# Who casts the weight chunks: ScalarE in the mixer, VectorE in the feed-forward part, with three smaller moves beside it

## The chip, the cores and the metric

One Trainium2 chip, one of its cores. The metric is the device time of the whole program in microseconds (us), median over runs. Engines are named as in the profile: PE is TensorE, PEld its weight loads, DVE VectorE, ACT ScalarE, POOL GpSimd, SP SyncE, whose queue issues nearly all DMAs. The granted clock is the share of full speed at which TensorE was allowed to run.

## The reference

Two layers over 528 tokens (16 meta tokens and 512 inputs) of width 1024, in float32. Each layer is a mixer and a convolutional feed-forward part:

```python
for l in range(2):
    xn = rms_norm(h, norm1_g)                    # mixer
    proj = xn @ w_in                             # q, k, v, gates of three attentions
    out_a, out_b, out_c = fox(...), mla(...), sliding_window(...)   # 8 heads each
    y = einsum('blnc,ncd->blnd', stack(out_a, out_b, out_c), w_branch)
    h = h + sum(sigmoid(gates) * y, axis=2) @ w_o
    u = rms_norm(h, norm2_g) @ w_up              # feed-forward part, 1024 -> 5632
    c = conv_b + sum(conv_w[i] * shift(u, i))    # width 3, causal
    gate, val = split(c, 2)
    h = h + (silu(gate) * val) @ w_down          # 2816 -> 1024
return h[:, 16:]
```

## The kernel before

**Layout.** Activations stand transposed: 128 features on the partitions, the 528 tokens along the row (`T`), one such tile for each 128 features. Every product with weights is a chain of 128x128 weight blocks; there are 1080 blocks per layer, 2160 in all, and they lie in DRAM in the order in which TensorE uses them.

**Split products.** A float32 product is made of three: `gemm` multiplies the high part of the weights (cast to fp32r, `wh`) with the high and the low part of the activations (`xh`, `xl`), and the low part of the weights (`wl`) with the high part of the activations. The 528 columns are two halves of 264, in two banks of PSUM, so a block is 6 matmuls. In the last layer columns that nothing reads are left out (`two_before`, `real`): the last products (`dn`) have halves of 248 and 264.

**The weight stream.** Eight blocks are a chunk, 128x1024 float32, 512 KB; there are 270. SP loads a chunk into one of `RAW = 2` places of `raw`, VectorE casts it to `wh` (`high_part`), GpSimd subtracts in four pieces to get `wl` (`chunk_low`), and TensorE uses it (`weights`). There are `SPLIT = 3` places of `wh` and `wl`, and the cast of a chunk is issued `AHEAD = 2` chunks before its use: at block n, VectorE's `advance` casts chunk n/8 + 2, after waiting for its load and for TensorE to have started chunk n/8 (`s_start`).

**The order of the mixer.** `mixer_plan` writes out one list for each engine. The position in it is the number of the weight block (488 in a mixer, so 61 chunks), and the steps of attention, norms and gates are put at positions by hand (`ORDER`, `BEGIN`, `LAG`); at one position they go by rank, and the block comes last, with rank 9. Each engine executes its own list in order. After the list come `w_o` (64 blocks), `up` (352) and `dn` (176).

**Norms.** The sum of squares over features is a matmul with ones (`stat`), then ScalarE guesses the root and VectorE refines it (`newton`). The input of a layer is scaled by the norm's weights on VectorE (`scale_input`, into `tmp`), cast on ScalarE (`high_input`), and subtracted on VectorE (`low_input`). In the first layer TensorE adds up the squares itself: `first_stat(k)` ahead of each of the first eight blocks of tile `ff`, and ScalarE squares h tile k only when the statistic of tile k-2 is done. In the second layer VectorE adds the squares (`sum_square`), and one `stat` follows.

**Before w_o.** When the whole list is done, ScalarE casts the eight tiles of `merged` (`mh`) and VectorE subtracts all eight (`ml`); TensorE's first block of `w_o` waits for the first `ml`.

**The start.** SP issues the first two tiles of h, the first constants, chunk 0, the other h tiles, chunk 1, then the rest of the constants and chunks 2 and 3. VectorE ticks `ready_made` at the end of its preamble; ScalarE waits for it before its list.

## Time and profile before

| | |
|---|---|
| median of 3 runs | 2052.18 us (2051.9 to 2056.09) |
| time of the profiled execution | 2050.07 us |
| its span, first to last instruction | 2048.3 us |
| mean granted clock | 0.992 |
| TensorE busy | 1974.3 us, 96% |

The profiled execution's time is 1.8 us more than its span, and 2.1 us under the median. Busy TensorE is not TensorE at its peak, since the ends of matmuls are modelled; start-to-start distances in the timeline tell the rate. A group of instructions is a row with its count, its busy time and the mean of one, and then the idle time of its engine just before it with what ended it.

### The profile page before, as it was taken

The numbers are of one execution on the slowest core, as the hardware profiler recorded it, in microseconds if no ns is written. First come the engines' busy times: TensorE is split into PE (matmuls) and PEld (weight loads), VectorE is DVE, ScalarE is ACT, GpSimd is POOL, SyncE is SP. The second block draws the span as 40 slices with busy tenths as digits, with TensorE's granted clock in tenths as the row PEclk, the third lists the DMA queues.
The fourth block names the chain that finished last, engine by engine and source line by source line (L and its number), as shares of the span: only waits on it lengthen the run. The fifth ranks groups of instructions, "written<-read, shape, count | busy, mean of one in ns | idle before, by whom it ended". The sixth has DMA issues, their size and how long they took to land.

```text
span 2048.3 us, 37777 instructions
## 1 busy us (share of the span) xinstructions
PE 1974.3 (96%) x15080; PEld 1876.6 (92%) x15080; DVE 1154.7 (56%) x2137; ACT 766.3 (37%) x1483; POOL 1019.4 (50%) x1306
## 2 busy tenths in 40 slices
PE   7899999999999999999998999999999999999999
PEld 7888898888999999999997888988889999999999
DVE  5665466677455665652256654666774656656411
ACT  5455566555232222220034555665552232222100
POOL 5745544444444444455467555444443445444543
PEclk9999999999999999999999999999999999999999
DMA  4212111111233323323332121111112323232332
GB/s 154 56 50 63 52 44 61 45 50 52 63 105 93 93 83 94 93 83 104 93 115 63 43 63 53 52 52 52 52 42 73 115 83 102 85 100 87 103 94 93
DMA packets 44803, 156.35 MB, mean 76 GB/s; under 512 B 5010, under 2 KB 5266, under 8 KB 44628
## 3 DMA queue, kind: packets, MB, share of 16 engines
q1 hardware_dynamic: 44484, 153.71, 24.8%
q8 instruction: 120, 1.97, 0.4%
q14 instruction: 55, 0.45, 0.1%
q10 hardware_dynamic: 144, 0.22, 0.0%
HBM read 149.58 MB, written 4.26 MB: 75 GB/s over the span
## 4 chain that ended last, share of the span: by engine, by line
PE 80%; DVE 10%; ACT 4%; issue 3%; POOL 2%; DMA 0%; DVEq 0%; ACTq 0%; SPq 0%; POOLq 0%
PE ps L1294 22%; PE ps L1297 21%; PE ps L1299 21%; PE ps L1528 5%; PE ps L1304 3%; DVE osum L1906 2%; PE ps L1435 1%; PE ps L1474 1%; DVE rstd L1619 1%; DVE ps L1876 1%; POOL wl L789 1%; PE ps L1480 1%; PE ps L1500 1%; DVE square L1614 1%; ACT square L987 1%
## 5 line engine op out<-in xcount | busy, mean ns | idle before, releaser
L789 POOL TENSOR_TENSOR wl<-raw,wh 128x256 fp32r<-128x256 f32 x1080 | 797.8, 771 | 723.5 <-DVE wh L1598 714.0
L1294 PE MATMUL ps<-xh,wh 128*128 128x264 f32 (+1 forms) x2880 | 810.6, 303 | 4.9 <-POOL wl L789 2.7
L1297 PE MATMUL ps<-xl,wh 128*128 128x264 f32 (+1 forms) x2880 | 762.9, 285 | 0.0
L1299 PE MATMUL ps<-xh,wl 128*128 128x264 f32 (+1 forms) x2880 | 584.1, 284 | 0.0
L1294 PEld LDWEIGHTS ps<-xh,wh 128*128 128x128 f32 x2880 | 545.5, 189 | 29.0 <-issue 16.0
L1297 PEld LDWEIGHTS ps<-xl,wh 128*128 128x128 f32 x2880 | 545.8, 190 | 15.4 <-issue 6.7
L1299 PEld LDWEIGHTS ps<-xh,wl 128*128 128x128 f32 x2880 | 450.4, 190 | 0.0
L1598 DVE CAST wh<-raw 128x1024 fp32r<-128x1024 f32 x270 | 200.2, 742 | 180.7 <-PE ps L1294 166.2
L1297 PE MATMUL ps<-al,wh 128*128 128x264 f32 (+1 forms) x704 | 184.9, 283 | 0.0
L1294 PE MATMUL ps<-ah,wh 128*128 128x264 f32 (+1 forms) x704 | 183.6, 283 | 0.0
L1898 DVE TENSOR_TENSOR ps<-ps,cst 128x128 f32<-128x128 f32 (+6 forms) x240 | 70.9, 296 | 189.0 <-PE ps L1480 135.8
L1528 PE MATMUL ps<-pt,vx 128*128 128x256 f32 (+5 forms) x448 | 144.7, 403 | 0.8 <-ACT pt L1214 0.7
L1299 PE MATMUL ps<-ah,wl 128*128 128x264 f32 (+1 forms) x704 | 141.5, 282 | 0.0
L1294 PEld LDWEIGHTS ps<-ah,wh 128*128 128x128 f32 x704 | 132.4, 188 | 0.0
L1297 PEld LDWEIGHTS ps<-al,wh 128*128 128x128 f32 x704 | 132.4, 188 | 0.0
L1214 ACT ACTIVATE pt<-ps 128x256 f32<-128x256 f32 (+5 forms) x224 | 78.0, 362 | 113.5 <-DVE ps L1898 112.3
L1262 ACT ACTIVATE cv<-ps,prm 128x528 f32<-128x528 f32 (+1 forms) x44 | 34.6, 787 | 209.0 <-DVE ps L1955 209.0
L1294 PE MATMUL ps<-oth,wh 128*128 128x264 f32 (+1 forms) x384 | 108.9, 305 | 2.2 <-DVE ssum L1706 0.9
L1299 PEld LDWEIGHTS ps<-ah,wl 128*128 128x128 f32 x704 | 109.3, 188 | 0.0
L1955 DVE TENSOR_TENSOR ps<-ps,rstd 128x528 f32<-128x528 f32 (+1 forms) x88 | 62.0, 705 | 80.5 <-PE ps L1299 80.4
L1297 PE MATMUL ps<-otl,wh 128*128 128x264 f32 (+1 forms) x384 | 100.8, 283 | 0.0
L1435 PE MATMUL ps<-xk,xq 96*128 96x144 f32 (+9 forms) x272 | 75.4, 303 | 18.3 <-POOLq L886 7.7
(183 smaller groups left out, 3213.3 us busy)
## 6 DMA issues: line engine op xcount, KB each, us to landing
raw<-weights SPq DMA_DIRECT2D x270, 512.0 KB, 3.6
h<-tokens SPq DMA_DIRECT2D x4, 528.0 KB, 6.6
h<-tokens SPq DMA_DIRECT2D x8, 264.0 KB, 5.4
residual<-h SPq DMA_DIRECT2D x8, 264.0 KB, 4.7
h<-residual SPq DMA_DIRECT2D x8, 264.0 KB, 5.9
out<-h SPq DMA_DIRECT2D x8, 256.0 KB, 4.9
cst<-constants SPq DMA_DIRECT2D x1, 1008.0 KB
extra<-positions SPq DMA_DIRECT2D x17, 4.1 KB
```

The costliest lines, as they stand in the source:

```text
L789: ins = nc.gpsimd.tensor_tensor(wl[c % SPLIT][:, part], raw[:, c % RAW, part], wh[c % SPLIT][:, part].bitcast(F32), ALU.subtract)
L1214: ins = nc.scalar.activation(pt[0:nk, i, 0:nq], bank[0:nk, 0:nq], ACT.Exp)
L1294: a = nc.tensor.matmul(out, a_hi, x_hi[:, sl], start=first, stop=False)
L1297: nc.tensor.matmul(out, a_hi, x_lo[:, sl], start=False, stop=False)
L1299: ins = nc.tensor.matmul(out, a_lo, x_hi[:, sl], start=False, stop=last)
L1304: ins = nc.tensor.matmul(half(slot, j), lhs, rhs[:, j * TH:(j + 1) * TH], start=first, stop=last)
L1435: ins = nc.tensor.matmul(bank[:, col:col + nk], xq[rows, i, e, q], xk[rows, i, e, k0:k0 + nk], start=True, stop=True)
L1528: ins = nc.tensor.matmul(heads_out[:, c:c + nq], vals[0:nk, :], pt[0:nk, i, 0:nq], start=t == 0, stop=t == 4)
L1598: nc.vector.tensor_copy(wh[c % SPLIT][:, :], raw[:, c % RAW, :]).then_inc(s_hi, 1)
L1898: nc.vector.tensor_tensor(sc, sc, cst[0:nk, a:a + n], ALU.add).then_inc(scores_masked.sem, scores_masked.tick((l, j, e, t)))
L1906: nc.vector.reciprocal(osum[:, a:a + T // 4], osum[:, a:a + T // 4]).then_inc(dve_step.sem, dve_step.tick((l, "recip", j, q)))
L1955: nc.vector.tensor_tensor(src[:, skip:T], src[:, skip:T], rstd[:, skip:T], ALU.mult).then_inc(up_scaled.sem, up_scaled.tick((l, t)))
```

## The change

- In the mixer, ScalarE casts the chunks, at the block steps of its own list; in `w_o`, `up` and `dn` VectorE does, as before. The first chunk of each engine's turn waits for the other's last one. Chunks 0 and 1 are still cast by VectorE, and it also makes the low part of chunk 0.
- ScalarE scales and casts the norms' input in one activation straight from h, and VectorE makes the low part with one operation from h, the norm's weights and `xh`. `tmp` and its scaling on VectorE are gone, for norm 1 and norm 2.
- In the first layer ScalarE squares into `merged`, with no wait for TensorE; VectorE adds the squares, and one `stat` replaces the eight. The first constants are loaded after all of h and chunks 0 and 1.
- The casts of `merged` and their low parts go in between: tile d's at the step that ends the next product tile, and only the last after the list.
- In the last layer's `dn`, a block is three matmuls of 512 columns into one bank, where it was six of 248 and 264.

```diff
@@ SP
             for k in range(0, KD, 2):
                 sp.dma_start(h[:, k:k + 2, :], H[:, k:k + 2, :]).then_inc(s_hin[k // 2], 16)
-                if k == 0:
-                    sp.dma_start(cst[:, 0:CC_FIRST], CST[:, 0:CC_FIRST]).then_inc(s_first, 16)
-                    load(0)
-            load(1)
+
+                if k <= 2:
+                    load(k // 2)
+            sp.dma_start(cst[:, 0:CC_FIRST], CST[:, 0:CC_FIRST]).then_inc(s_first, 16)
@@ ScalarE
             def high_input(l, k):
-                act.wait_ge(scaled.sem, scaled.at(l, "n1", k))
-                copy(xh[:, k, :], tmp[:, k % 2, :]).then_inc(high_ready.sem, high_ready.tick((l, "n1", k)))
+                nc.scalar.activation(xh[:, k, :], h[:, k, :], ACT.Identity,
+                                     scale=prm[:, l, PC_N1 + k:PC_N1 + k + 1]).then_inc(
+                    high_ready.sem, high_ready.tick((l, "n1", k)))
+            def merged_cast(l, d):
+                act.wait_ge(gate_used.sem, gate_used.at(l, "sum", MLA, d))
+                copy(mh[:, d, :], merged[:, d, :]).then_inc(merged_high.sem, merged_high.tick((l, d)))
             for k in range(KD):
+                if k % 2 == 0:
+                    act.wait_ge(s_hin[k // 2], 16)
                 high_input(0, k)
-                if k >= 2:
-                    act.wait_ge(stat_ready.sem, stat_ready.at(0, "part", k - 2))
-                nc.scalar.activation(hsq[:, k % 2, :], h[:, k, :], ACT.Square).then_inc(
+                nc.scalar.activation(merged[:, k, :], h[:, k, :], ACT.Square).then_inc(
                     residual_squared.sem, residual_squared.tick((-1, "dn", k)))
                 for s in plan["act"]:
+                    if s[0] == "block":
+                        n = l * LB + n_blocks
+                        n_blocks += 1
+                        if n % BLK == 0:
+                            c = n // BLK + AHEAD
+                            if first:
+                                act.wait_ge(s_hi, c)
+                                first = False
+                            act.wait_ge(s_raw[c % RAW], 16 * (c // RAW + 1))
+                            if c >= SPLIT:
+                                act.wait_ge(s_start, c - SPLIT + 2)
+                            copy(wh[c % SPLIT][:, :], raw[:, c % RAW, :]).then_inc(s_hi, 1)
+                    elif s[0] == "done" and s[1].kind == "y":
+                        br, d = s[1].m
+                        if br == MLA and d != Y_LAST[0]:
+                            merged_cast(l, Y_LAST[Y_LAST.index(d) - 1])
@@ TensorE
+            def gemm_in_bank(n, out, x_hi, x_lo, first, last):
+                a_hi, a_lo = weights(n)
+                a = nc.tensor.matmul(out, a_hi, x_hi, start=first, stop=False)
+                if n % BLK == 0:
+                    a.then_inc(s_start, 1)
+                nc.tensor.matmul(out, a_hi, x_lo, start=False, stop=False)
+                return nc.tensor.matmul(out, a_lo, x_hi, start=False, stop=last)
                         if t.kind == "ff":
-                            if l == 0:
-                                first_stat(k)
                             pe.wait_ge(low_ready.sem, low_ready.at(l, "n1", k))
@@ VectorE
             def low_input(l, k):
                 dve.wait_ge(high_ready.sem, high_ready.at(l, "n1", k))
-                nc.vector.tensor_tensor(xl[:, k, :], tmp[:, k % 2, :], xh[:, k, :].bitcast(F32),
-                                        ALU.subtract).then_inc(low_ready.sem, low_ready.tick((l, "n1", k)))
+                nc.vector.scalar_tensor_tensor(out=xl[:, k, :], in0=h[:, k, :], scalar=prm[:, l, PC_N1 + k:PC_N1 + k + 1],
+                                               in1=xh[:, k, :].bitcast(F32), op0=ALU.mult, op1=ALU.subtract).then_inc(
+                    low_ready.sem, low_ready.tick((l, "n1", k)))
+            for k in range(KD):
+                low_input(0, k)
+                if k == 0:
+                    high_part(0)
+                    dve.wait_ge(s_hi, 1)
+                    nc.vector.tensor_tensor(wl[0][:, :], raw[:, 0, :], wh[0][:, :].bitcast(F32), ALU.subtract).then_inc(
+                        s_lo, 1)
+                elif k == 3:
                     high_part(1)
+                if k >= 4:
+                    sum_square(-1, "dn", k - 4)
+            for k in range(KD - 4, KD):
+                sum_square(-1, "dn", k)
                     if s[0] == "block":
-                        advance(l, n_blocks)
                         n_blocks += 1
```

## Rows read from the trace of the kernel before

**Rows 1.** The page: busy time of each engine, share of the span, instructions.
```profile
PE 1974.3 (96%) x15080; PEld 1876.6 (92%) x15080; DVE 1154.7 (56%) x2137; ACT 766.3 (37%) x1483; POOL 1019.4 (50%) x1306
```
**Rows 2.** Stretches, one in the first mixer, one in `up`: length, busy time by engine.
```profile
400.00:500.00 100.00, 94.77 (x668) 85.03 (x667) 74.93 (x156) 54.20 (x105) 46.12 (x52) 1.00 0.18 54
...
800.00:920.00 120.00, 120.00 (x984) 120.00 (x983) 71.25 (x102) 27.64 (x40) 58.73 (x83) 1.00 0.30 88
```
**Rows 3.** The chain of work that ended last, share of the span by engine.
```profile
PE 80%; DVE 10%; ACT 4%; issue 3%; POOL 2%; DMA 0%; DVEq 0%; ACTq 0%; SPq 0%; POOLq 0%
```
**Rows 4.** TensorE's waits: line, what it waited for, us in total, times, longest.
```profile
PE ps L1435 <- POOLq L886: 7.7, 3, 3.9
...
PE ps L1294 <- DVE ml L1916: 5.1, 2, 2.5
...
PE ps L1474 <- ACT ptm L1193: 4.7, 6, 1.0
```
**Rows 5.** Groups of instructions by line, shapes kept apart: busy us, mean ns.
```profile
L1598 DVE CAST wh<-raw 128x1024 fp32r<-128x1024 f32 x270 | 200.2, 742 | 180.7 <-PE ps L1294 166.2 <-DMA raw<-weights 13.3 <-DVE merged L1755 0.2
...
L1643 DVE TENSOR_TENSOR hsum<-hsum,sq 128x528 f32<-128x528 f32 x21 | 15.4, 735 | 2.1 <-ACT sq L1243 2.0
...
L970 ACT ACTIVATE xh<-rawt 128x528 fp32r<-128x528 f32 x32 | 20.4, 636 | 123.0 <-DVE rawt L1628 122.5 <-DVE rawt L1936 0.6
...
L1262 ACT ACTIVATE cg<-ps,prm 128x528 f32<-128x528 f32 x22 | 17.4, 793 | 45.8 <-DVE ps L1955 45.8
...
L977 ACT ACT_TABLE_LOAD x12 | 15.4, 1283 | 0.2
...
L1075 ACT ACTIVATE gsb<-gsb 128x1056 f32<-128x1056 f32 x12 | 12.8, 1081 | 8.9 <-DVE gsb L1739 8.9
...
L789 POOL TENSOR_TENSOR wl<-raw,wh 128x256 fp32r<-128x256 f32 x1080 | 797.8, 771 | 723.5 <-DVE wh L1598 714.0 <-POOL xq L802 2.5 <-POOL xk L877 1.0
```
**Rows 6.** Timeline of the start: start us, length us, idle time before in brackets.
```profile
5.32 1.27 DVE L1628 TENSOR_SCALAR rawt<-h,prm 128x528 f32<-128x528 f32 x2 [4.02 <-DMA h<-tokens]
...
7.08 0.69 DVE L1598 CAST wh<-raw 128x1024 fp32r<-128x1024 f32 x1 [0.48 <-DMA raw<-weights]
...
12.02 0.56 PE L1294 MATMUL ps<-xh,wh 128*128 128x264 f32 x1 [2.75 <-POOL wl L789]
...
14.79 1.96 PE L1304 MATMUL ps<-sq,cst 128*128 128x264 f32 x4
...
26.17 1.30 DVE L1598 CAST wh<-raw 128x1024 fp32r<-128x1024 f32 x2
...
33.14 0.39 PE L1294 MATMUL ps<-xh,wh 128*128 128x264 f32 x1 [0.80 <-DVE krt L1718]
...
34.70 1.16 PE L1304 MATMUL ps<-sq,cst 128*128 128x264 f32 x4
```
**Rows 7.** Timeline of TensorE: blocks of the last `dn`, then a 512-column product.
```profile
1990.14 0.28 PE L1294 MATMUL ps<-ah,wh 128*128 128x248 f32 x1
...
1992.99 0.28 PE L1294 MATMUL ps<-ah,wh 128*128 128x248 f32 x1
...
424.47 0.39 PE L1474 MATMUL ps<-xq,xk 97*128 97x512 f32 x1
...
425.17 0.29 PE L1294 MATMUL ps<-xh,wh 128*128 128x264 f32 x1
```
**Rows 8.** Second layer's `w_o`: its first matmul, and the stretch just after.
```profile
1620.05 0.35 PE L1294 MATMUL ps<-mh,wh 128*128 128x250 f32 x1 [2.53 <-DVE ml L1916]
...
1621.00:1624.40 3.40, 3.40 (x18) 3.40 (x17) 3.40 (x7) 0.00 (x0) 0.00 (x0) 0.51 0.99 317
```
**Rows 9.** Timeline around two of the mixer's stalls of TensorE.
```profile
319.95 0.39 PE L1474 MATMUL ps<-xq,xk 97*128 97x256 f32 x1 [0.83 <-ACT ptm L1193]
...
432.04 1.36 DVE L1598 CAST wh<-raw 128x1024 fp32r<-128x1024 f32 x1
...
434.16 0.18 PE L1474 MATMUL ps<-xq,xk 97*16 97x16 f32 x1 [0.75 <-ACT pt L1214]
```

More of the change, by code:

```diff
@@ L446, in build @@
     lrstd = hsum
-    tmp, hsq = rawt, sq
+    hsq = sq
     vt = sb("vt", [P, TK])
@@ L822, in _ @@
             pool.sem_inc(zeroed.sem, zeroed.tick((0, 0)))
-            for c in range(AHEAD):
+            for c in range(1, AHEAD):
                 chunk_low(c)
@@ L1233, in _ @@
                             heads_copied.sem, heads_copied.tick((l, j, e)))
-                for d in Y_LAST:
-                    act.wait_ge(gate_used.sem, gate_used.at(l, "sum", MLA, d))
-                    copy(mh[:, d, :], merged[:, d, :]).then_inc(merged_high.sem, merged_high.tick((l, d)))
+                merged_cast(l, Y_LAST[-1])
                 def square_residual(which, k):
@@ L1246, in _ @@
                 for k in range(KD):
+                    act.wait_ge(residual_updated.sem, residual_updated.at(l, "wo", k))
+                    nc.scalar.activation(xh[:, k, :], h[:, k, :], ACT.Identity,
+                                         scale=gain[:, l, PC_N2 + k:PC_N2 + k + 1]).then_inc(
+                        high_ready.sem, high_ready.tick((l, "n2", k)))
                     square_residual("wo", k)
-                    act.wait_ge(scaled.sem, scaled.at(l, "n2", k))
-                    copy(xh[:, k, :], tmp[:, k % 2, :]).then_inc(high_ready.sem, high_ready.tick((l, "n2", k)))
                 logarithms()
@@ L1575, in _ @@
                     slot = DN_SLOTS[m]
+                    if real:
+                        if m % 2 == 0:
+                            pe.wait_ge(up_freed.sem, up_freed.at(l, 2 * FT - 4 + m // 2))
+                        out = last_bank(m)
+                        for k in range(FT):
+                            if m == 0:
+                                pe.wait_ge(act_low.sem, act_low.at(l, k))
+                            ins = gemm_in_bank(l * LB + n_blocks, out, ah[:, k, real:T], al[:, k, real:T], k == 0,
+                                               k == FT - 1)
+                            n_blocks += 1
+                        ins.then_inc(tile_ready.sem, tile_ready.tick((l, "dn", m)))
+                        continue
                     if m < 4:
@@ L1598, in high_part @@
                 nc.vector.tensor_copy(wh[c % SPLIT][:, :], raw[:, c % RAW, :]).then_inc(s_hi, 1)
+            turns = {"mixer": True}
             def advance(l, i):
@@ L1602, in advance @@
                 if n % BLK == 0:
+                    if turns["mixer"]:
+                        dve.wait_ge(s_hi, n // BLK + AHEAD)
+                        turns["mixer"] = False
                     high_part(n // BLK + AHEAD)
```

74 lines of the change are left out of this document (33 added, 41 removed).

## The prediction

> **What bounds the kernel now.** I read the page first: TensorE is busy 1974.3 us of a span of 2048.3 [rows 1], so all its idle time together is 74.0 us, and nothing that the change does to another engine can give more than that unless it shortens TensorE's own work. The stretches come next [rows 2]: in `up` TensorE is busy 120.00 of 120.00 us, with VectorE at 59%; in the mixer it is busy 94.77 of 100, with VectorE at 75% and ScalarE at 54%. So the feed-forward part is bound by TensorE's instructions alone, and the engines that feed TensorE matter only in the two mixers and at the start. The chain that ended last says the same: 80% TensorE, 10% VectorE, 4% ScalarE, 2% GpSimd [rows 3]. The waits of TensorE [rows 4] name no single cause: the reader should see many stalls of about 1 us, behind VectorE, ScalarE and GpSimd alike, and one that the change addresses by name, 5.1 us in two stalls behind `ml`. The timeline is then read at the start, at `w_o` and in the last `dn`.
>
> **The start.** Before, h is there at 5.32 and chunk 0 at 7.08; GpSimd makes chunk 0's low part, and TensorE's first block begins at 12.02 [rows 6]. After, ScalarE makes `xh` 0 straight from h (0.64 as a plain cast, 0.79 as the activation with a scale per partition [rows 5]; I take 0.7), VectorE subtracts (0.74) at about 6.8, casts chunk 0 (0.74), and makes its low part: twice the columns of a 0.735 us operation, less its fixed part, 1.3 us. That ends at 8.8: 3.2 us earlier. The next condition is block 16, which needs chunk 2. Its cast waits for `ready_made`, behind VectorE's whole preamble. Counted from 8.8: seven low parts, eight additions and the cast of chunk 1 at 0.74 are 11.8 us, then 0.5 for the gains: 21.1. Overlap of neighbours takes some off, GpSimd working on chunk 1 beside it puts some on; I take 21.2. ScalarE casts chunk 2 (1.05, priced below) and GpSimd makes it low in 4 x 0.771 = 3.1 us [rows 5]: TensorE can start block 16 at about 25.4. TensorE itself is ready earlier: from 8.8, 16 blocks at 0.72 us and one statistic of about 1.0 are 12.5, and the first blocks run at half speed, as before, where the first two took 14.79 - 12.02 = 2.77 us [rows 6], 1.3 more than two at 0.72. Twice that, 2.6, gives 23.9. Before, chunks 2 and 3 were cast at 26.17, and block 16 began at 33.14, for eight statistics stood in the way [rows 6]. That is 7.7 us earlier.
>
> What is late next is the root of norm 1. ScalarE reaches it after the casts of chunks 2 and 3, at 23.5; a table load of 1.28 and six operations of 0.64 (copy, logarithm, exponential, square, then copy and square of the first tile) are 5.1 us [rows 5] and end at 28.7, where TensorE does that tile's statistic. Before, that statistic began at 34.70 [rows 6]. So from here the whole schedule runs 6.0 us earlier, and TensorE waits there some 2 us that it did not wait before. The stall behind GpSimd (L886, two of nearly 4 us, one in each layer [rows 4]) stays: its chain moves with the statistic. I take 6.0 for the start. The lower bound is 3.2, the first block's gain alone; the upper 8.
>
> **w_o.** Each layer's first block of `w_o` waits 2.5 us for `ml`, since VectorE begins the eight subtractions only when its list is done. After, the first seven are done in between, and only the last is behind the list; TensorE needs that one 14 blocks, 10 us, later. The added work per product tile of 4 blocks (2.9 us) on VectorE is one subtraction of 0.7, beside two operations of 0.7, so it does not pace. Gain 5.1 us [rows 4]. In the second layer the stall is followed by 3.4 us at a granted clock of 0.51 [rows 8], which is half speed, 1.7 us of work lost. Without the stall I take 1.3 of it back. Together 6.4; bounds 5.1 and 6.8.
>
> **The last dn.** Four blocks take 1992.99 - 1990.14 = 2.85 us, 0.7125 a block, six matmuls [rows 7]. Three matmuls of 512 columns in a row are in the trace too: from 424.47 to the next instruction of another kind at 425.17, 0.70 us. The columns are the same, 1536, so only what each matmul costs beside its columns is saved: 0.0125 us by this row. Resolution is 0.01 at both ends, and the three there are of other products. 176 blocks x 0.0125 = 2.2 us. Nothing is the lower bound. From above: 248 and 264 columns at 2.4 GHz are 0.640 us for the block, so 0.0725 stands beside the columns; halving it gives 0.036, or 6.4 us. I take 2.8, near the row. The Trainium skill (TensorE: Matmul & The Clock Gate, on the 56 ns gap) puts that cost at about 2.5 ns for a matmul; by it the sum would be 176 x 3 x 0.0025 = 1.3 us, an estimate. The trace has more beside the columns than that, so the two disagree.
>
> **The casts.** VectorE loses 122 casts, two mixers of 61, at 0.742 us: 90 us of work [rows 5]. ScalarE gains them. The nearest row is an activation without a scale per partition over 1056 columns, 1.081 us; for 1024 I take 1.05, so 128 us. The stretch of 100 us in [rows 2] holds some ten of them: ScalarE goes from 54% to about 65%, VectorE from 75% to 67%; neither becomes the bound by its sum. What counts is who stands in line behind a cast. ScalarE's cast at block n waits for TensorE to start block n, as VectorE's did, and then exponentials, key copies and root guesses wait up to 1.05 us; on VectorE, masks, maxima and refinements stop waiting 0.74 us, or 1.36 as in [rows 9]. For a gain: the cast of 1.36 us at 432.04 is followed by the stall of 0.75 at 434.16 [rows 9]; I count seven like it in both layers, about 5 us. For a loss: the stalls behind `ptm` (4.7 us in six) have ScalarE as the late engine already, busy with the copies of the next job; the one at 319.95 [rows 9] is the start of the job at block 250, two blocks behind the chunk boundary 248, so its 0.83 becomes up to 1.9. Some five places per layer are like that. A stall also brings half clock with it in places, as in [rows 8]. I take 2 us slower for both mixers, between 6 faster (all seven, and a clock drop) and 12 slower (1.05 us exposed at ten of the 122 casts, and one clock drop).
>
> **Norm weights inside the cast.** Norm 2 and the second layer's norm 1 lose 24 scalings on VectorE, and ScalarE's casts get 0.1 longer. TensorE has no stall there, in either place; one block of cover, 0.7 us, is more than what any link changes. Nothing. Had that cover gone, the low part would come at most 0.2 us later per tile.
>
> **The sum.** -6.0 - 6.4 - 2.8 + 2.0 = -13.2 us. Against the profiled execution's 2050.07 that is 2036.9. Its time was 2.1 us under the median of 2052.18, and a median of the changed kernel may lie above its profile too, so I take half of that on top: 2038.
>
> **Rivals.**
> - *The start gives little.* If the preamble on VectorE is stretched by GpSimd or by late DMAs (the first constants now come after 3.4 MB), `ready_made` slips, with it chunk 2, and only the first block's 3.2 us are kept, or less. 2040 to 2043. For it: 16 operations in a row on one engine. Against: chunk 0 was there 1.8 us after h [rows 6]; at that pace the five pieces of half a megabyte ahead of the constants are there by 15, before they are wanted.
> - *The casts on ScalarE help.* If removing VectorE's casts mends the seven stalls and ScalarE has room, the mixers give 6 us: 2029. For it: the same cast takes 0.69 us at 7.08 and 1.36 at 432.04 [rows 6, 9], and what it waits for there, GpSimd may wait for elsewhere. Against: GpSimd is on 2% of the chain [rows 3]. The Trainium skill (SBUF — State Buffer, on the engine ports) says that GpSimd and a VectorE copy in its two-port mode lock each other out, and that ScalarE's ports are its own; by it the move frees both engines, and it speaks for this rival. That the cast's length varies agrees with it.
> - *ScalarE becomes the late engine of the attention.* Three banks rotate among scores and maxima, so a score tile that ScalarE frees 1.05 us late holds up the third one behind it. The other parts give 15.2 us; it decides against the change once the mixers lose more than that and 4 us, 0.16 us for each of the 122 casts. At 0.2 they lose 24: 2050.07 - 15.2 + 24 = 2059. For it: stalls behind ScalarE exist already [rows 4]. Against: ScalarE would still idle a third of the mixer [rows 2].
> - *The wide matmuls give nothing*, at the same rate per column: 2040.
>
> **How the numbers follow.** The forecast, 2032 to 2043 with its own bounds, has 0.55 (the first and fourth rivals' milder forms lie in it). The helping casts: 0.2, 2024 to 2032. A weak start and exposed casts together in part: 0.12, 2043 to 2048. ScalarE late: 0.13, 2048 and up, more than half of it beyond 2052+4. The range 2024 to 2049 leaves 0.06 below and about 0.12 above. Within 0.2% is 2048.1 to 2056.3, about what a measurement of this kernel can tell from no change: 0.07. Faster: 0.86. Slower: 0.07.
>
> **What would show it.** First block of TensorE near 8.8, and the first tile's statistic near 28.7. No idle time before `w_o`'s first matmul, and no half clock behind it in the second layer. Start-to-start of a block in the last `dn` between 0.68 and 0.71. ScalarE's casts near 1.05 us; TensorE's idle time between 70 us and the end of each mixer within 2 us of before. If the waits of TensorE behind `pt`, `ptm` and `sq` grow by more than 15 us together, the prediction is wrong in its sign.

## The result, and the profile after

The changed kernel takes 2068.23 us (median of 5 runs, 2067.23 to 2072.54); the kernel before, run beside it, 2051.9 us. The ratio is 1.0083, with a 95% interval from 1.0066 to 1.0099: 16 us slower, where the prediction had 14 us faster. It is wrong in its sign, and 19 us beyond its range.

The profiled execution took 2067.81 us, with a span of 2066.0, against 2048.3 before. Its page, busy time by engine, answers to [rows 1]; under it the stretches of [rows 2]:

```profile
PE 1976.0 (96%) x14524; PEld 1854.0 (90%) x14524; DVE 1067.4 (52%) x1992; ACT 885.3 (43%) x1605; POOL 1012.2 (49%) x1302
```
```profile
400.00:500.00 100.00, 93.37 (x651) 83.99 (x650) 64.55 (x137) 61.64 (x112) 43.88 (x48) 0.98 0.15 45
800.00:920.00 120.00, 120.00 (x983) 120.00 (x983) 70.70 (x101) 27.62 (x40) 58.89 (x84) 1.00 0.31 93
```

VectorE did lose 87 us and ScalarE did gain 119. In the mixer ScalarE is busy 62% and VectorE 65%, nearly as forecast, and neither is full. `up` is as it was. What differs is TensorE in the mixer: 93.37 us instead of 94.77, at a granted clock of 0.98 instead of 1.00. Here are its waits (line, what it waited for, us in total, times, longest), to set against [rows 4]:

```profile
PE ps L1343 <- DVE rawt L1801: 13.2, 10, 2.5
...
PE ps L1464 <- POOLq L889: 7.4, 2, 3.8
PE ps L1503 <- ACT ptm L1222: 6.9, 6, 1.7
...
PE ps L1464 <- ACT xk L973: 6.7, 2, 3.4
...
PE ps L1503 <- ACT ptm L1225: 4.5, 6, 1.1
```

The 5.1 us behind `ml` are gone. `ptm` has 11.4 us instead of 5.6, `xk` 6.7 instead of 3.0, `rawt` 13.2 instead of 9.0: many small growths, behind ScalarE and behind VectorE.

**Where the time went.** I set matching instructions of TensorE against each other, above all the statistics (line 1304 before, 1343 after) and the first matmul of each chunk. After minus before: -4.1 us at the first tile's statistic (30.60 against 34.70), +10.5 at the end of the first mixer, +7.8 behind its `w_o`, +7.8 up to the end of the first `dn`, +11.3 at block 24 of the second layer, +24.3 at the end of the second mixer, +20.1 behind its `w_o`, +17.7 at the end of the span. So the start gave 4.1, the two `w_o` 6.9 and the last `dn` 2.4, 13.4 us together, where 15.2 were forecast. The two mixers took 31, where 2 were forecast.

**The start.** The timeline answers to [rows 6] (start us, length us, idle time before in brackets):

```profile
5.49 1.28 ACT L1004 ACT_TABLE_LOAD   x1 [5.49 <-DMA h<-tokens]
6.78 0.73 ACT L1004 ACTIVATE xh<-h,prm 128x528 fp32r<-128x528 f32 x1
...
9.04 1.22 DVE L1725 TENSOR_TENSOR wl<-raw,wh 128x1024 fp32r<-128x1024 f32 x1
...
10.41 0.56 PE L1324 MATMUL ps<-xh,wh 128*128 128x264 f32 x1 [10.41 <-DVE wl L1725]
...
12.98 5.02 POOL L792 TENSOR_TENSOR wl<-raw,wh 128x256 fp32r<-128x256 f32 x4 [6.15 <-DVE wh L1640]
...
13.84 1.24 DVE L1675 SCALAR_TENSOR_TENSOR xl<-h,prm,xh 128x528 fp32r<-128x528 f32 x1
...
23.50 2.00 ACT L973 ACTIVATE wh<-raw 128x1024 fp32r<-128x1024 f32 x2 [7.33 <-DVE nsink L1736]
...
25.52 1.28 ACT L980 ACT_TABLE_LOAD   x1
...
27.56 0.36 PE L1324 MATMUL ps<-xh,wh 128*128 128x264 f32 x1 [2.43 <-POOL wl L792]
...
30.60 1.16 PE L1343 MATMUL ps<-sq,cst 128*128 128x264 f32 x4 [1.34 <-ACT sq L1058]
```

There is a table load that the forecast did not have. It stands in front of ScalarE's first activation, and so behind the wait for h; it ends at 6.78. The first block begins at 10.41 instead of 8.8. While GpSimd makes the low part of chunk 1 (5.02 us instead of 3.1), VectorE's operations with two inputs take 1.24 us instead of 0.76, so the small tiles are ready at 23.5 instead of 21.2, and the rest of the chain moves with them.

**w_o and the last dn.** The first matmul of the second layer's `w_o` has no idle time before it, and where [rows 8] had a clock of 0.51 the clock is 1.00:

```profile
1641.81 0.28 PE L1324 MATMUL ps<-mh,wh 128*128 128x250 f32 x1
```
```profile
1642.00:1646.00 4.00, 4.00 (x36) 4.00 (x35) 3.40 (x5) 0.65 (x1) 0.44 (x1) 1.00 0.85 276
```

In the last `dn` six blocks of three matmuls go from 1995.00 to 1999.19, 0.698 us a block, where [rows 7] had 0.7125:

```profile
1995.00 0.39 PE L1335 MATMUL ps<-ah,wh 128*128 128x512 f32 x1
...
1999.19 0.39 PE L1335 MATMUL ps<-ah,wh 128*128 128x512 f32 x1
```

**The casts.** By groups, ScalarE's cast has the forecast length, the casts left to VectorE are shorter than in [rows 5], and GpSimd's low parts are as long as before (774 ns, 771 before):

```profile
L792 POOL TENSOR_TENSOR wl<-raw,wh 128x256 fp32r<-128x256 f32 x1076 | 799.4, 774 | 774.7 <-DVE wh L1640 434.0 <-ACT wh L973 333.3 <-POOL xq L805 1.9
...
L973 ACT ACTIVATE wh<-raw 128x1024 fp32r<-128x1024 f32 x122 | 128.5, 1054 | 59.0 <-PE ps L1324 50.4 <-DVE nsink L1736 7.3 <-DMA raw<-weights 0.4
...
L1640 DVE CAST wh<-raw 128x1024 fp32r<-128x1024 f32 x148 | 102.6, 693 | 140.4 <-PE ps L1335 64.1 <-PE ps L1324 64.0 <-DMA raw<-weights 12.2
```

So the length of one cast was forecast rightly. The mixers' loss must come from where the casts stand.

### The profile page after: what moved, and what is told of

It reads as the page before. It is cut to its first block and busy times, and to the rows that moved or that the text cites. A ratio compares the mean times of both kernels' runs of the same rounds, so it can differ in the third digit from the quotient of the medians.

```text
span 2066.0 us, 36684 instructions
## 1 busy us (share of the span) xinstructions
PE 1976.0 (96%) x14524; PEld 1854.0 (90%) x14524; DVE 1067.4 (52%) x1992; ACT 885.3 (43%) x1605; POOL 1012.2 (49%) x1302
## 5 line engine op out<-in xcount | busy, mean ns | idle before, releaser
L1640 DVE CAST wh<-raw 128x1024 fp32r<-128x1024 f32 x148 | 102.6, 693 | 140.4 <-PE ps L1335 64.1
L973 ACT ACTIVATE wh<-raw 128x1024 fp32r<-128x1024 f32 x122 | 128.5, 1054 | 59.0 <-PE ps L1324 50.4
L1503 PE MATMUL ps<-xq,xk 97*16 97x16 f32 (+17 forms) x288 | 79.6, 294 | 16.5 <-ACT ptm L1222 6.9
L1327 PE MATMUL ps<-al,wh 128*128 128x264 f32 x352 | 93.0, 285 | 0.0
L1324 PE MATMUL ps<-ah,wh 128*128 128x264 f32 x352 | 92.9, 284 | 0.0
L1961 DVE RECIPROCAL osum<-osum 128x132 f32<-128x132 f32 x96 | 88.5, 953 | 8.1 <-ACT oraw L973 7.8
L1343 PE MATMUL ps<-sq,cst 128*128 128x264 f32 (+1 forms) x224 | 63.8, 411 | 17.8 <-DVE rawt L1801 13.2
```

The source lines that it names most:

```text
L973: return nc.scalar.activation(out, in_, ACT.Copy)
L1324: a = nc.tensor.matmul(out, a_hi, x_hi[:, sl], start=first, stop=False)
L1327: nc.tensor.matmul(out, a_hi, x_lo[:, sl], start=False, stop=False)
L1343: ins = nc.tensor.matmul(half(slot, j), lhs, rhs[:, j * TH:(j + 1) * TH], start=first, stop=last)
L1503: nc.tensor.matmul(out, xk[rows, i, e, keys], xq[rows, i, e, q], start=True, stop=False)
L1640: nc.vector.tensor_copy(wh[c % SPLIT][:, :], raw[:, c % RAW, :]).then_inc(s_hi, 1)
```

## The experiments

The theories at first: A, ScalarE's 1.05 us per cast makes it the late engine. B, several parts lose together. C, the cast's wait for TensorE, standing in ScalarE's list, holds back what is behind it. Below, "boundary" is TensorE's first matmul on a new chunk, every eight blocks, and a "stretch" is the time from one boundary to the next, named by its first block.

**1. Casts back on VectorE** (`e1_dve_casts`: the changed kernel without this one part).
```diff
-  ScalarE, in the mixer: copy(wh[c % SPLIT], raw[c % RAW]) at each boundary
+  VectorE: advance(l, n_blocks) at each "block" of its list, as before the change
```


> The changed kernel with the mixer's chunks cast by VectorE again, at VectorE's own block steps; all else as in the change. Theory A (ScalarE is the late engine of the attention, and the 122 casts on it are the whole loss): the mixers return to what they took before, so 27 us come back, 2041 us, and TensorE's idle time in each mixer falls by about 8 us. Theory B (the loss is of several parts: squares and norms on ScalarE at the start, interleaved casts of merged too): less than 15 us come back, 2053 us or more.

Measured 2040.02 us, ratio to the kernel before 0.9938 (0.9915 to 0.9961). The parts that were left gain 11 us, and both mixers are within 3 us of before, as theory A had it. The other parts do not hurt: B falls.

**2. Casts alone** (`e2_act_casts_only`: the kernel before with this one part).
```diff
+  ScalarE, in the mixer: the cast at each boundary
-  VectorE: advance(l, n_blocks) in the mixer
```


> The kernel before with one part of the change: the mixer's chunks cast by ScalarE. Theory A: all the loss is here, without the gains: 27 us slower than before, 2078 us. Theory B: no more than 12 us slower, 2063 us.

2083.24 us, ratio 1.0157 (1.0126 to 1.0188), 32 us slower where A had 27. Both ways round the casts cost 28 to 32 us, 0.23 to 0.26 us for each of the 122.

**3. The wait alone** (`e5_wait_only`: as 1, and ScalarE waits at each boundary for TensorE's start, but casts nothing).
```diff
+  if n % BLK == 0 and c >= SPLIT:
+      act.wait_ge(s_start, c - SPLIT + 2)
```


> As the run with the casts back on VectorE, but ScalarE keeps its wait for TensorE's start of the chunk at each boundary, and does nothing there. Theory C (the wait is the harm): 10 us or more slower than the run without the wait. Theory A: within 3 us of it.

2043.65 us, 3.6 us more than 1: just beyond A's 3 us and far from C's 10. The wait by itself is an eighth of the loss.

**4. The cast two and four blocks later** (`e3_late`, `e8_late4`: the changed kernel with `n % BLK == 2`, `== 4`).
```diff
-  if n % BLK == 0:
+  if n % BLK == 2:        # e8_late4: == 4
```


> The changed kernel, ScalarE's cast of a chunk put two blocks later in its list (at n % 8 = 2), so that TensorE has started the chunk that the cast waits for before ScalarE comes to it. Theory C (the harm is the wait in ScalarE's queue: 50 us of ScalarE's idle time end with TensorE starting a block, and what stands behind waits too): half or more of the loss goes, 2055 us or less. Theory A (the harm is the 1.05 us of work itself, wherever it stands): within 5 us of the changed kernel, 2063 to 2073.

> The changed kernel with ScalarE's casts four blocks behind the boundary. ScalarE has the same 128.5 us of casts, but no wait for TensorE in its queue, and GpSimd's low part is 2.9 us later. The cast two blocks behind gave 2058.8. If the wait and what stands next to the boundary is what costs, 2048 to 2060; if ScalarE's time costs wherever it stands, 2060 to 2070; if the casts come too late for the next chunk (1.1 of 5.8 us of cover are left for cast and low part, 4.2 us, before the boundary), TensorE waits behind wl and it is above 2070.

2058.79 us and 2078.88 us. The first lies between the forecasts of A and C and settles nothing by itself: three of its ten runs took about 2052 us and the other seven 2057.7 to 2060.5, and the profiled one, 2052.06, is of the three. ScalarE has the same work in both. Here are the mixers' stalls of TensorE by releaser, both layers, each from its block 24 on, summed from the timeline:

```
us of idle TensorE      ScalarE  VectorE  GpSimd's queue   all
before                   17.9     26.8        7.7          52.5
after                    32.0     28.2        7.4          67.7
1: casts on VectorE      19.0     26.5        7.7          53.2
4: two blocks later      21.8     25.2       11.7          59.6
4: four blocks later     14.9     22.3       37.1          75.5
5: busy, no cast         23.1     27.9        7.2          58.2
6: VectorE, 1 later      18.8     29.6       11.0          59.4
```

("all" has 0.8 and 1.2 us behind GpSimd's own operations too, in the two kernels of run 4.)

With the cast four blocks late the stalls behind ScalarE are even fewer than before, so theory A as it stood loses ground: 128 us of work more on ScalarE cost nothing behind ScalarE where they stand in another place. It is not settled by this, since TensorE waits so long for others here that ScalarE may catch up meanwhile; `e11_spared` settles it (run 8). The time is above 2070, as the third forecast had it, but not for its reason: TensorE hardly waits behind `wl`. Instead GpSimd's list, which waits for each cast, is late with what stands behind the low part:

```profile
PE ps L1464 <- POOLq L889: 37.0, 9, 6.8
```

**5. ScalarE busy, no cast moved** (`e6_busy`: as 3, and then five copies of 128x3 into a scratch tile that nobody reads).
```diff
+  act.wait_ge(s_start, c - SPLIT + 2)
+  for i in range(5):
+      copy(waste[:, 3 * i:3 * i + 3], prm[:, 0, 0:3]).then_inc(s_waste, 1)
```


> Left as in the version with all casts on VectorE (2040.0 us), but at each block boundary of the mixer ScalarE waits for TensorE's start, as for a cast, and then does five copies of 128x3 (by its small operations about 0.2 us each, 1.0 us together), which nobody waits for. VectorE casts and GpSimd's low part stay where they were. If what costs is ScalarE's time alone (the copies, exponentials and root guesses behind it come 1 us later), this gives most of the loss: 2060 to 2068. If it is the later cast that pushes GpSimd's low part onto VectorE's work, or the tables and masks that VectorE now reaches earlier, this stays near the kernel with the wait alone, 2043.7: 2042 to 2050.

2049.67 us: 9.6 more than 1, at the upper edge of the second forecast and far below the first. The wait and ScalarE's time at the boundary are a third of the loss, and 3.6 of the 9.6 are the wait's, by run 3. But the substitute is weaker than it was meant to be. Each copy lasts 0.19 us, and they overlap: all 610 keep ScalarE busy for 70.3 us, 0.58 at each of the 122 boundaries, where a cast takes 1.05.

```profile
L975 ACT ACTIVATE waste<-prm 128x3 f32<-128x3 f32 x610 | 70.3, 192 | 59.0 <-PE ps L1326 50.7 <-DVE nsink L1734 7.3
```

**6. VectorE casts one block later** (`e7_vector_late1`).
```diff
-  advance(l, n_blocks)                      # casts at n % BLK == 0
+  if n % BLK == 1:
+      high_part(n // BLK + AHEAD)
```


> All casts on VectorE, but in the mixers one block (0.72 us) later than the boundary, so that GpSimd's low part begins some 0.7 us later than with the casts at the boundary, and ScalarE has none of it. If the later low part collides with VectorE's work at bad places, the mixers lose 5 us or more: 2045 to 2055. If ScalarE's time is all of it, no change beyond 3 us from 2040.0: 2037 to 2043.

2050.24 us: 10.2 more than 1, with nothing on ScalarE. In the mean over the 122 boundaries the cast ends 2.42 us behind the boundary in 1, 2.92 in the changed kernel, 3.06 here. A later cast costs by itself. It does not cost at the same places, though: 4.4 us of the loss stand in the stretch from block 40, both layers together, where TensorE waits longer for GpSimd's queue, and there the changed kernel loses nothing.

**7. Both together** (`e13_busy_late`: 5 and 6 in one kernel).

> Both substitutes together: ScalarE waits at the boundary and does 0.96 us of copies that nobody waits for (alone 9.6 us slower than 2040.0), and VectorE casts one block late (alone 10.2 us slower), so that the cast ends 3.1 us behind the boundary, as in the changed kernel. If ScalarE's hold and the later low part are the two halves of the loss and add up, 2059 to 2064; if they act in the same places and strengthen each other, up to 2070; if one hides the other, 2050.

2061.23 us, 21 more than 1: the two add up (9.6 + 10.2). The sum is three quarters of the loss with no cast on ScalarE, but it is not three quarters rebuilt: 4.5 us of it are again at block 40. What the substitutes do at the places where the changed kernel loses is in run 8.

**8. Where the loss is made.** I cut the traces at the boundaries. Of 61 stretches a layer most are the same to 0.05 us in the changed kernel and in 1; these are the five with the largest differences in both layers (us over 1, first and second layer):

```
stretch of block     120          288          312          328          352          all 122
after            0.93  2.54   2.31  2.24   3.49  3.43   0.94  0.91   0.87  0.92       28.3
e10_five         1.09  1.12   2.31  3.30   1.96  3.41   0.95  0.92   0.87  0.93       16.4
e11_spared      -0.16 -0.15  -1.03  1.46   0.02  0.01   0.01 -0.01   0.01  0.00       -1.9
```

and in six stretches (blocks 32, 56, 144, 240, 336, 376) the changed kernel is faster, by up to 0.7 us each. Some stretches differ as much in one layer alone: 3.5 us at block 248 of the first and 2.9 at block 192 of the second, of which 0.7 and 1.0 are idle time and the rest a granted clock of 0.79 and 0.90 instead of 1.00, and 1.9 and 1.6 at blocks 8 and 16 of the second, which come below. Of the 28.3 us, 18.3 are idle time of TensorE, and 10.0 the same work at a lower clock. So the next two kernels divide the casts by place. `e10_five`: ScalarE casts at these five places only, ten of the 270 casts. `e11_spared`: VectorE keeps 18 casts of each mixer, ScalarE takes 43.
```diff
+  BY_SCALAR = {15, 36, 39, 41, 44}          # e11_spared: set(range(61)) less 18 places
+  ScalarE: at a boundary k in BY_SCALAR, wait for the cast before it if that was VectorE's, and cast
+  VectorE: the same for all others
```


> From the version with all casts on VectorE (2040.0 us), ScalarE takes only five of the 61 casts of each mixer: those begun at blocks 120, 288, 312, 328 and 352. Cut at the chunk boundaries, the trace of the changed kernel is longer than that version's in these stretches by 0.9, 2.3, 3.5, 0.9 and 0.9 us in the first layer and 2.6, 2.2, 3.4, 0.9 and 0.9 in the second, 18.5 us together. If each loss is made where its cast stands, these ten casts alone give it: 2056 to 2061. If the loss comes from ScalarE's total load, ten of 122 casts give a twelfth of 28 us, 2.3: 2040 to 2044.

> The complement, with more spared: VectorE keeps the 18 casts of each mixer whose stretch was longer by some 0.2 us or more in either layer, ScalarE takes the other 43, 86 in all. If the losses are local, what is left are the gains, in the stretches of blocks 32, 56, 144, 240, 336 and 376 (0.4, 0.5, 0.7, 0.7, 0.3, 0.6 us a layer) and two waits more at each change of hands: 2033 to 2040. If ScalarE's load as such costs, 86 of 122 casts give 70% of 28 us: 2060.

2059.65 us and 2034.34 us, ratios 1.0040 (1.0025 to 1.0055) and 0.9920 (0.9905 to 0.9935), both as forecast for a local loss. Ten casts cost 19.6 us in the medians (16.4 in the trace, which is of the shortest run); 86 casts at other places cost nothing, and that kernel has the lowest median measured here. The other 26 casts stayed with VectorE in both kernels. The loss is local. It is not a matter of load; by groups, `e11_spared`:

```profile
L974 ACT ACTIVATE wh<-raw 128x1024 fp32r<-128x1024 f32 x86 | 90.7, 1055 | 35.3 <-PE ps L1324 34.6
```

TensorE's idle time in a stretch tells more than its length, since the clock is not in it. Where nothing was changed it repeats to about 0.02 us between kernels (us, first and second layer, worked out from the timeline):

```
stretch of block       120         288         312         328         352      8, second
1                  0.15 0.26   1.42 1.53   0.45 0.65   0.75 0.80   0.00 0.00     1.16
3: wait            0.20 0.33   1.42 1.52   1.29 1.35   0.75 0.80   0.00 0.00     1.17
5: wait, copies    0.77 0.94   1.42 1.52   1.85 1.92   1.17 1.20   0.13 0.17     1.87
6: VectorE later   0.46 0.57   1.70 1.80   0.39 0.45   0.74 0.79   0.00 0.00     1.16
7: both            1.05 1.19   1.71 1.81   1.85 1.92   1.15 1.20   0.12 0.17     1.87
after              1.08 1.18   3.33 3.38   2.39 2.45   1.64 1.67   0.60 0.64     3.05
```

At blocks 328 and 352 only ScalarE's time acts: the wait and the later cast do nothing, copies of 0.58 us give up to half of what the cast gives, and TensorE waits for `pt` and for `vx`, which stand behind it. At block 120, where it waits for `ptm`, the copies give more than half and the later cast the rest. At block 288 ScalarE's time does nothing and the later cast a little. At block 312 and at block 8 the cast gives more than its length.

**9. What acts at block 288.** In the kernel of 1, VectorE casts 0.54 us behind the boundary, and of VectorE's chain of six operations for the next tile, a refinement of two steps and four products, only the first meets GpSimd's low part:

```profile
374.32 2.80 POOL L792 TENSOR_TENSOR wl<-raw,wh 128x256 fp32r<-128x256 f32 x4 [9.25 <-DVE wh L1630]
...
376.58 1.10 DVE L1650 SCALAR_TENSOR_TENSOR square<-ssum,square 128x528 f32<-128x528 f32 x1
...
377.72 0.71 DVE L1653 SCALAR_TENSOR_TENSOR rstd<-square,rstd 128x528 f32<-128x528 f32 x1
...
378.56 0.75 DVE L1862 SCALAR_TENSOR_TENSOR q<-rawt,gain,rstd 64x528 f32<-64x528 f32 x1
...
379.32 0.70 DVE L1865 TENSOR_TENSOR q<-krr,rstd 32x528 f32<-32x528 f32 x1
380.05 0.77 DVE L1862 SCALAR_TENSOR_TENSOR q<-rawt,gain,rstd 64x528 f32<-64x528 f32 x1
...
380.83 0.70 DVE L1865 TENSOR_TENSOR q<-krr,rstd 32x528 f32<-32x528 f32 x1
```

In the changed kernel ScalarE is at its root guess when the boundary comes, and casts 2.73 us behind it. The low part then lies on that chain:

```profile
381.32 1.05 ACT L973 ACTIVATE wh<-raw 128x1024 fp32r<-128x1024 f32 x1
...
382.16 0.70 DVE L1664 SCALAR_TENSOR_TENSOR square<-ssum,square 128x528 f32<-128x528 f32 x1
...
382.45 4.45 POOL L792 TENSOR_TENSOR wl<-raw,wh 128x256 fp32r<-128x256 f32 x4 [11.85 <-ACT wh L973]
382.89 1.12 DVE L1667 SCALAR_TENSOR_TENSOR rstd<-square,rstd 128x528 f32<-128x528 f32 x1
...
384.13 1.03 DVE L1875 SCALAR_TENSOR_TENSOR q<-rawt,gain,rstd 64x528 f32<-64x528 f32 x1
...
385.17 1.14 DVE L1878 TENSOR_TENSOR q<-krr,rstd 32x528 f32<-32x528 f32 x1
386.34 1.13 DVE L1875 SCALAR_TENSOR_TENSOR q<-rawt,gain,rstd 64x528 f32<-64x528 f32 x1
...
387.48 1.53 DVE L1878 TENSOR_TENSOR q<-krr,rstd 32x528 f32<-32x528 f32 x1
...
389.95 0.56 PE L1464 MATMUL ps<-xk,xq 96*128 96x264 f32 x1 [3.33 <-ACT xk L973]
```

The chain begins 3.56 us behind the boundary in both kernels. Its six operations take 6.65 us instead of 4.73 and it ends 1.9 us later, which is all that TensorE's idle time grew by; the rest of the stretch's 2.31 is the clock. GpSimd's four take 4.45 instead of 2.80. Both sides slow each other; ScalarE's `xk`, which TensorE is said to wait for, is only the last link. The Trainium skill (SBUF — State Buffer, on the two separate sides) says that a VectorE operation with two inputs in SBUF and a GpSimd operation that reads SBUF lock each other out for a whole instruction; these rows agree, with 0.70 become 1.12 where a GpSimd piece of 0.7 us is in the way.

The kernel of run 6 has no cast on ScalarE, and its low part begins 2.28 us behind this boundary, between 1.31 in 1 and 3.85 in the changed kernel. It meets two operations of the chain:

```profile
376.24 3.74 POOL L792 TENSOR_TENSOR wl<-raw,wh 128x256 fp32r<-128x256 f32 x4 [8.41 <-DVE wh L1630]
...
378.26 1.12 DVE L1653 SCALAR_TENSOR_TENSOR rstd<-square,rstd 128x528 f32<-128x528 f32 x1
...
379.50 1.03 DVE L1864 SCALAR_TENSOR_TENSOR q<-rawt,gain,rstd 64x528 f32<-64x528 f32 x1
```

The chain ends 0.29 us later than in 1, and TensorE's idle time is 0.28 us longer. So the collision without ScalarE lengthens this stall; how much it gives at 3.85 us behind the boundary is read from the rows of the changed kernel only.

`e14_one_late3` has all casts on VectorE, but this one three blocks later:
```diff
+  if n_blocks // BLK == 36:
+      if n % BLK == 3: high_part(n // BLK + AHEAD)
+  else:
       advance(l, n_blocks)
```


> All casts on VectorE (2040.0 us), but the one of block 288 in each layer three blocks later, so that GpSimd's low part begins some 3.5 us behind the boundary, as with the cast on ScalarE (3.97), and not 1.42. If the later low part is the cause at that place, the stretch from block 288 to 296 gets 1 to 2.3 us longer in each layer, VectorE's two refinements and four products there take 1.0 to 1.5 us instead of 0.7, and the whole is 2042 to 2045. If ScalarE's own time is the cause there, no change: 2039 to 2041, apart from one cast of 0.7 us in VectorE's chain.

2041.27 us (2039.91 to 2043.77), the stretch 1.15 and 0.71 us longer, its idle time 0.75 and 0.70. The cast came later than meant, 6.6 us behind the boundary and inside the chain, so the first operation missed the low part and the last one met it:

```profile
378.07 0.70 DVE L1650 SCALAR_TENSOR_TENSOR square<-ssum,square 128x528 f32<-128x528 f32 x1
...
381.13 0.69 DVE L1630 CAST wh<-raw 128x1024 fp32r<-128x1024 f32 x1
...
381.85 0.77 DVE L1867 SCALAR_TENSOR_TENSOR q<-rawt,gain,rstd 64x528 f32<-64x528 f32 x1
381.90 3.82 POOL L792 TENSOR_TENSOR wl<-raw,wh 128x256 fp32r<-128x256 f32 x4 [15.33 <-DVE wh L1630]
382.63 1.13 DVE L1870 TENSOR_TENSOR q<-krr,rstd 32x528 f32<-32x528 f32 x1
```

The last operation is 0.43 longer than in 1, the first 0.40 shorter, and the cast itself takes 0.72: 0.75 together, the growth of the idle time. The one collision took the place of the other. So this run shows that a cast inside the chain costs its length; it does not test the later low part, and the 1.9 us were not rebuilt in this way.

**10. What acts at block 312.** With all casts on VectorE, ScalarE has loaded the tanh table and done the first tanh before the boundary. In the changed kernel the cast stands ahead of them in its list and waits there:

```profile
409.63 1.06 ACT L973 ACTIVATE wh<-raw 128x1024 fp32r<-128x1024 f32 x1 [3.27 <-PE ps L1324]
...
410.71 1.28 ACT L1104 ACT_TABLE_LOAD   x1
...
412.00 2.06 ACT L1104 ACTIVATE gsb<-gsb 128x1056 f32<-128x1056 f32 x2
...
416.16 2.10 PE L1343 MATMUL ps<-sq,cst 96*128 96x264 f32 x4 [2.39 <-DVE rawt L1801]
```

3.27 us of waiting, in which a load and a tanh would have fitted, and then all of it on the path to `rawt`. The table of run 8 divides it: over 1, the wait alone gives 0.84 us of idle time in the first layer and 0.70 in the second, with copies of 0.58 us behind it 1.40 and 1.27, with the cast 1.94 and 1.80. The same pair stands at block 8 of the second layer, ahead of the root of its first norm, where in 1 the load was done before the boundary:

```profile
1054.17 1.06 ACT L973 ACTIVATE wh<-raw 128x1024 fp32r<-128x1024 f32 x1 [3.05 <-PE ps L1324]
1055.25 1.28 ACT L980 ACT_TABLE_LOAD   x1
```

TensorE's idle time there is 3.05 us instead of 1.16 (1.17 with the wait alone, 1.87 with the copies), and the next eight blocks run at a clock of 0.80 instead of 1.00, 1.6 us more. `e16_tanh_first` is `e10_five` with this one cast moved behind the next tanh:
```diff
+  k == 39: keep the cast for later
   nc.scalar.activation(gates, gates, ACT.Tanh, scale=0.5)
+  cast it here
```


> The version with ScalarE's five casts per mixer (2059.7 us), but its cast of block 312 stands behind the next tanh instead of ahead of it. The tanh's gate is there before TensorE reaches block 312, so the table load (1.28) and tanh (1.08) go into ScalarE's wait. If the wait in the list is the cause at that place, the stretch from block 312 to 320 loses what it had gained (2.0 and 3.4 us): 2053 to 2056. If the cast's 1.05 us as such is the cause, at most 0.5 us a layer: 2058.5 to 2060.

2050.80 us (2047.06 to 2056.24), 8.9 less than `e10_five` (2055.84 to 2061.24) and more than was forecast. The stretch lost all it had gained (1.96 to -0.06, 3.41 to -0.19), 5.6 us in both layers, and the cast itself is still ScalarE's. The profiled executions don't show the medians' difference: that of `e10_five` was its shortest run, this one the longest of its own, and in it the stretches of blocks 88, 120 and 248, where nothing was changed, are up to 2.9 us longer. So the stretch is the evidence here; the median is more than it gives.

**11. The start, and a best version.** `e9_table_first` is 1 with the table of logarithms loaded at the head of ScalarE's list; `e12_six_table` gives ScalarE in addition the six casts where the changed kernel was faster; `e15_spared_table` is `e11_spared` with the table first.
```diff
   act.dma_start(prm[:, :, :], PRM[:, :, :]).then_inc(s_prm, 16)
+  logarithms()
```


> All casts on VectorE, and ScalarE loads the table of logarithms at the head of its list, before it waits for h. The load of 1.28 us at 5.49 goes into the shadow of h's transfer and the second load, before the root of norm 1, is gone. If both lie on the path: first block of TensorE 1.3 us earlier and the first tile's statistic 1.3 to 2.5 earlier, 2037.5 to 2039. If the path there is VectorE's and GpSimd's (chunk 1 and 2), only 0 to 1.3 us: 2038.7 to 2040.

> The version with the table loaded first (2036.6 us), and ScalarE takes only the six casts of each mixer in whose stretch the changed kernel was faster. If those gains are local too, 2 x 3.2 us less: 2030.2, range 2028 to 2034. If they came from a cast elsewhere, or each change of hands costs as much as it gives, 2035 to 2041.

> ScalarE takes 43 of the 61 casts of each mixer (2034.3 us with them), and its first table load stands at the head of its list (3.4 us less in the version where VectorE casts all). If start and mixers are independent: 2031, range 2029 to 2033. If the preamble's shift changes what meets in the mixers: 2033 to 2037.

2036.63, 2034.78 and 2036.01 us. The table first gives 3.4 us in the medians, but less than that is its own: in the trace TensorE's first block begins at 9.41 and its block 16 at 26.58, both 0.8 us earlier than in 1, where 1.3 were forecast, and the first tile's statistic at 28.53, 1.2 earlier. The rest of the traces' difference is 3.1 us at blocks 88 and 192 of the first layer, with the same idle time and a higher clock. The other two were expected at 2030 and 2031 if the gains added up. They did not; `e15_spared_table` lies in its second forecast. The six local gains are there in `e12_six_table` (up to 0.6 us each), but they are given back elsewhere. Windows over the same eight blocks (248 to 256 of the first layer), first in `e9_table_first`, then in `e12_six_table`:

```profile
308.95:322.07 13.12, 12.00 (x86) 10.34 (x84) 5.27 (x12) 9.57 (x25) 7.99 (x10) 1.00 0.26 82
```
```profile
310.24:326.49 16.25, 14.86 (x85) 12.56 (x84) 5.46 (x12) 9.80 (x25) 9.01 (x11) 0.79 0.22 67
```

Idle time is 1.1 and 1.4 us; the work went from 12.00 to 14.86 us, with the granted clock at 0.79 instead of 1.00. Four versions stand between 2034 and 2037 us, and their ranges overlap; `e11_spared` has the lowest median, 2034.34, 17 us under the kernel before, and no run tells the four apart.

## Why the prediction was wrong

**The step that failed** is the price of the casts for both mixers, 2 us, and its bound "between 6 faster ... and 12 slower (1.05 us exposed at ten of the 122 casts, and one clock drop)". The two mixers lost 31 us, 28 of them by the casts (run 1). The bound takes the cast's own length as the most that a place can lose. That holds at blocks 120, 328 and 352, where TensorE's idle time grew by 0.6 to 0.9 us, and at block 248, the place that the prediction names, where its 0.83 became 1.53. It fails elsewhere, since three things go with the cast that I had priced at nothing or nearly so:
- *The wait moves too.* I wrote that ScalarE's cast waits for TensorE as VectorE's did, and named what is behind it, but took the cast's length as the delay. At block 312 it waited 3.27 us, and a table load of 1.28 and a tanh of 1.09 came behind it: 1.9 us of idle time in each layer, shown by moving the one cast (run 10). At block 8 of the second layer it was 1.9 us again.
- *The cast comes when ScalarE comes to it.* At block 288 it starts 2.2 us later than VectorE's. GpSimd's low part follows it and meets VectorE's chain: 1.9 us of idle time in each layer. That the one cast does it is shown by `e10_five`, where it is as large; that it is the collision is read from the rows of run 9, and run 6 shows the collision without ScalarE at 0.3 us. The prediction said nothing of GpSimd's new hours.
- *Clock.* The mean granted clock fell from 0.992 to 0.986, 12.6 of the 28 us over the version with VectorE's casts (0.014 of a span of 2066.0 is 28.9 us, 0.008 of 2037.5 is 16.3); by stretches it is 10.0, and the other 18.3 are idle time. I had one drop, under 2 us.

That the bound counts ten places, and that ten casts made 19.6 of the 28 us, is luck: the ten were taken from stalls behind `ptm`, and only block 120 of the five is one of those.

**The rivals.** "ScalarE becomes the late engine of the attention" had the sign, the place and nearly the time (2059), with 0.13, and its price of 0.2 us per cast was measured at 0.23. As a matter of steady load it is refuted: 86 casts cost nothing. In places it is there: TensorE's waits behind `ptm` and `pt` went from 10.3 to 18.5 us in the mixers, and ScalarE's time alone gives part of that (run 5). "The casts on ScalarE help" is right at six places a layer, which give 0.2 to 0.7 us each. The rule that spoke for it, that the move frees VectorE and GpSimd from each other (the Trainium skill, SBUF — State Buffer, on the two separate sides), changed nothing in the mean: GpSimd's pieces took 774 ns, 771 before.

**The sign I would have read.** I had said that waits behind `pt`, `ptm` and `sq` growing by over 15 us would show it. They grew by 8 in the mixers (13.4 to 21.8), and the sign turned all the same: `rawt`, `xk` and `vx` took 10 more, and the clock the rest.

**The start** was forecast at -6.0 and measured at -4.1, in its bounds. Its first block came 1.6 us earlier, not 3.2. Two terms were missing: the table load behind the wait for h (1.28, of which run 11 gives back 0.8), and the stretch of VectorE's operations to 1.24 beside GpSimd's 5.02 us, which the rival of a weak start had in words. Block 16 began at 27.56 instead of 25.4, the statistic at 30.60 instead of 28.7.

**w_o** gave 2.7 and 4.2, 6.9 together, against 6.4: a tenth above its upper bound, but right in both its pieces, the stall and the clock behind it. **The last dn** gave 2.4 against 2.8; 0.698 us a block is just under the 0.70 of the row, and 176 x 0.0145 is 2.6. **Norm weights inside the cast** cost nothing in the feed-forward part, as said. In the second layer's first stretches 3.5 us went, which the prediction put at nothing. They belong to the casts, since ScalarE's casts of blocks 0 and 8 now stand ahead of the layer's root: in `e10_five` and `e11_spared`, where VectorE makes these, they are not there.

**The chances** add up to 1.00 without the 0.06 that the prediction gives to a time below 2024.

**What stays open.** At block 288 no run made the low part as late as the changed kernel has it without ScalarE's cast, so 1.6 of the 1.9 us of idle time rest on the rows alone. At blocks 120, 328 and 352 the cause is read from the substitutes, at about half the length of a cast; there, too, no single cast was moved. What made the granted clock fall in one kernel and not in another is not known: the stalls do not tell it, since it also changed between kernels with the same idle time.

## What to carry to other kernels

An instruction that is moved to another engine takes its waits along, and in a list that runs in order a wait costs what stands behind it. So price a move place by place: when does the new engine reach it, what is behind it, and who starts when it ends. A load that fits on average can cost 1% at ten places, and the cut at fixed work (chunk boundaries) finds these places in two traces, if idle time and clock are told apart in each piece. Moving the casts only where they are harmless gave the lowest median here. And a substitute that shall take an engine's time has to be measured itself: five copies of 0.19 us kept ScalarE for 0.58, not 0.96.

## What the runs showed of the hardware

The same eight blocks with the same idle time, 1.2 us, took 11.85 us of work at a granted clock of 1.00 in `e10_five` and 14.79 at 0.79 in `e16_tanh_first` (blocks 248 to 256 of the second layer, whose casts VectorE makes in both); stretches of blocks 88, 192, 248 and 280 move by 1.5 to 3 us between kernels in this way. Gains of half a microsecond at a stall are below that, and should be looked for in the stretch, in its idle time above all, not in the total. A table load of 1.28 us stands directly in front of the activation that needs it, behind that one's wait (5.49 to 6.77 at the start), unless it is asked for earlier: in `e9_table_first` it begins at 1.17 us.
